# One-core encoder layer: four places for down weights, loads of experts 2 and 3 moved ahead, rows turned on VectorE, and one uniform expert loop

## What is computed

```python
x = x + mix @ w_out                        # after retention and differential attention
h = rmsnorm(x, norm_ffn)
# every token picks 1 of 4 groups, then 2 of the group's 4 experts (16 experts in all)
for e in its two experts:
    hid = silu(h @ w_gate[e]) * (h @ w_up[e])      # 1024 -> 512
    x  += weight[e] * (hid @ w_down[e])            # 512 -> 1024
gate = sigmoid(rmsnorm(x, norm_ple) @ w_ple_gate)
x = x + gate * (p @ w_ple_proj)
return rmsnorm(x, norm_final)
```

## Time and profile before

| | us |
|---|---|
| median of 3 runs | 639.49 (637.5 to 639.87) |
| the profiled execution, its time | 636.99 |
| the profiled execution, its span | 635.1 |
| TensorE busy | 589.0 (93%) |
| VectorE busy | 209.7 (33%) |
| ScalarE busy | 199.0 (31%) |
| GpSimd busy | 51.1 (8%) |

### The profile page before, as it was taken

One profiled execution on the slowest core, in us unless ns is written; L12 is line 12 of the kernel. 1 busy time (PEld: TensorE's weight loads), 2 busy tenths in 40 slices (PEclk: granted clock), 3 DMA queues, 4 the chain that ended last, 5 costly groups with the idle time before them and its releaser, 6 DMA issues.

```text
span 635.1 us, 9546 instructions
## 1 busy us (share of the span) xinstructions
PE 589.0 (93%) x3496; PEld 386.2 (61%) x3497; DVE 209.7 (33%) x460; ACT 199.0 (31%) x435; POOL 51.1 (8%) x89
## 2 busy tenths in 40 slices
PE   9999999999999999975769999999999987998994
PEld 9988777878988999974223333333333332335883
DVE  4521365456344342265101111011011010164753
ACT  5622254545443543240100010010010010073774
POOL 0000000000000000001101211211212211110000
PEclk9999999999999999995789999999999999998998
DMA  9852214213220249737994799999999999934001
GB/s 310 221 203 99 71 63 133 67 32 101 68 67 1 67 160 419 316 136 296 362 418 183 296 418 425 422 418 422 419 422 422 420 421 421 393 120 179 34 33 66
DMA packets 47232, 151.52 MB, mean 239 GB/s; under 512 B 7896, under 2 KB 27232, under 8 KB 34656
## 3 DMA queue, kind: packets, MB, share of 16 engines
q1 hardware_dynamic: 43520, 139.77, 56.3%
q0 software_dynamic: 3392, 11.02, 4.4%
q10 hardware_dynamic: 288, 0.29, 0.2%
HBM read 141.62 MB, written 9.45 MB: 238 GB/s over the span
## 4 chain that ended last, share of the span: by engine, by line
PE 83%; DMA 5%; DVE 4%; issue 3%; SPq 2%; ACT 2%; DVEq 0%; POOL 0%; ACTq 0%; POOLq 0%
PE bank L1622 19%; PE bank L1348 13%; PE bank L1349 12%; PE bank L1350 12%; PE bank L1648 10%; DMA ring_dn<-in_w_down 5%; PE bank L1430 2%; PE bank L1681 2%; SPq L586 2%; PE bank L1608 2%; PE bank L1403 2%; PE bank L1356 1%; PE bank L1634 1%; PE bank L1567 1%; PE bank L1444 1%
## 5 line engine op out<-in xcount | busy, mean ns | idle before, releaser
L1622 PE MATMUL bank<-ring_gu,rowsT 128*64 128x512 f32 (+1 forms) x800 | 144.7, 602 | 6.4 <-DMA ring_gu<-in_w_up 2.8
L1622 PEld LDWEIGHTS bank<-ring_gu,rowsT 128*64 128x64 f32 (+1 forms) x800 | 43.9, 128 | 92.4 <-issue 88.1
L1648 PE MATMUL bank<-ring_dn,hidT 128*64 128x512 f32 (+1 forms) x400 | 74.7, 607 | 9.8 <-issue 5.2
L891 ACT ACTIVATE silu_g<-bank 128x256 f32<-128x256 f32 x20 | 7.7, 384 | 221.8 <-PE bank L1622 221.8
L1087 DVE TENSOR_TENSOR w_lo<-w_raw,w_hi 128x2048 fp32r<-128x2048 f32 x17 | 39.0, 2293 | 76.7 <-ACT w_hi L752 64.9
L1246 DVE TENSOR_TENSOR hid<-silu_g,bank 128x256 f32<-128x256 f32 x20 | 8.4, 421 | 147.9 <-ACT silu_g L891 147.9
L1348 PE MATMUL bank<-w_hi,hT_hi 128*128 128x256 f32 x192 | 55.5, 289 | 0.8 <-issue 0.6
L1349 PE MATMUL bank<-w_lo,hT_hi 128*128 128x256 f32 x192 | 54.3, 283 | 0.0
L1350 PE MATMUL bank<-w_hi,hT_lo 128*128 128x256 f32 x192 | 54.3, 283 | 0.0
L1348 PE MATMUL bank<-hT_hi,w_hi 128*128 128x512 f32 x128 | 50.9, 397 | 0.1
L1648 PEld LDWEIGHTS bank<-ring_dn,hidT 128*64 128x64 f32 (+1 forms) x400 | 21.0, 128 | 48.4 <-issue 42.3
(11 more groups left out here) (217 smaller groups left out, 892.7 us busy)
## 6 DMA issues: line engine op xcount, KB each, us to landing
ring_gu<-in_w_gate SPq DMA_DIRECT2D x32, 1024.0 KB, 12.3
ring_gu<-in_w_up SPq DMA_DIRECT2D x32, 1024.0 KB, 15.3
ring_dn<-in_w_down SPq DMA_DIRECT2D x16, 2048.0 KB, 21.5
w_raw<-in_w_in SPq DMA_DIRECT2D x13, 1024.0 KB, 5.0
w_raw<-in_w_out SPq DMA_DIRECT2D x4, 1024.0 KB, 4.9
ple_gate_raw<-in_w_ple_gate SPq DMA_DIRECT2D x1, 4096.0 KB, 28.9
yg<-y_rows SPq DMA_DIRECT2D x8, 512.0 KB, 7.2
xr<-in_x SPq DMA_DIRECT2D x4, 512.0 KB, 8.8
```

Of the source, the lines that this page charges most:

```text
L1622: last = T.matmul(b_gu[q * BLK + t:q * BLK + t + n, :], rowsT[:, k % 4, k // 4, t:t + n], ring_gu[s][:, :, k, q * UC:(q + 1) * UC], start= ...
L1648: last = T.matmul(b_dn[q * BLK + t:q * BLK + t + n, :], hidT[:, kf % 2, kf // 2, t:t + n], ring_dn[s][:, kf, q * (D // 2):(q + 1) * (D // 2)],
```

## The change

It does these things.

- `ring_dn` gets a fourth place (`DN_AT` has four addresses, `GU_AT` three). Down of expert e + 1 is now loaded with gate-up of expert e. Gate-up 2 and down 3 are issued right behind the stores of `h2`, down 2 once the tables are ready. SP's loop over experts is written out, and in it each expert has gate-up e, then down e + 1, which waits for `dn_done` of the last block of expert e - 3. `ple_proj` is loaded behind the experts, `ple_gate_raw` in four pieces, and `gfin` last.
- The four row transposes and the two hidden transposes of TensorE, and the copies out of their banks, are gone. VectorE turns 32 by 32 squares instead: one instruction for a block's rows (`rows_turned`) and eight for its hidden values (`hidden_turned`). For this, `h2_rows` has four rows of 256 values for each token in place of two of 512, and a block is gathered by two indirect transfers.
- TensorE's code ahead of the loop and behind it is gone. The loop runs for all blocks and one turn more: turn t does `gate_up` of block t - 1 and `down` of block t - 2. In the first turn the code for `down` matches no copy. `one_of` is a chain of comparisons, one after the other, over six copies for `gate_up` and eight for `down`.
- The transposes of `p` stand behind the routing products, and `pair_weights` is done by VectorE after the first block's rows.

The diff, cut to its core:

```diff
+GU_AT = [107.75, 155.75, 16]
+DN_AT = [139.75, 187.75, 48, 0]
+N_GU, N_DN = len(GU_AT), len(DN_AT)
+
+
+CODE_DN, CODE_GU_LOADS, CODE_DN_LOADS = 8, 128, 1024
+NO_GU, NO_DN = 2 * N_GU, 2 * N_DN
...
-            def load_gu(e, slot, half):
+            def load_gu(e, half):
 
                 ks = slice(half * KD // 2, (half + 1) * KD // 2)
                 for n, w in enumerate((w_gate, w_up)):
-                    src = w[bass.ds(e, 1)].rearrange("o (q p j) f -> p (o q) j f", p=P, q=2)
-                    sp.dma_start(ring_gu[slot][:, n, ks, :], src[:, half]).then_inc(s_gu[slot][half], 16)
-
-            def load_dn(e, slot):
-                sp.dma_start(ring_dn[slot][:].rearrange("p (q j) n -> p q j n", q=2),
-                             w_down[bass.ds(e, 1)].rearrange("o (q p j) n -> p (o q) j n", p=P, q=2)).then_inc(s_dn[slot], 16)
+                    src = w[e].rearrange("(p h j) f -> p h j f", p=P, h=2)
+                    sp.dma_start(ring_gu[e % N_GU][:, n, ks, :], src[:, half]).then_inc(s_gu[e % N_GU][half], 16)
+
+            def load_dn(e):
+                sp.dma_start(ring_dn[e % N_DN][:],
+                             w_down[e].rearrange("(p j) n -> p j n", p=P)).then_inc(s_dn[e % N_DN], 16)
+
+            def blocks_through(e):
+                return sp.value_load(cum_i[0:1, e:e + 1], min_val=1, max_val=MAX_BLOCKS)
 
             for e in range(2):
-                load_gu(e, e, 0)
-                load_gu(e, e, 1)
-                load_dn(e, e)
-
-            sp.wait_ge(x1_add, NT * (OUT_UNITS - 1))
-            sp.dma_start(p_sb[:], p.rearrange("(t p) c -> p t c", p=P)).then_inc(s_pple, 16)
-            sp.dma_start(h2_rows[2 * SEQ:2 * SEQ + 2].rearrange("r (a c) -> (r a) c", c=BLK),
-                         small_tab[BLK:BLK + 2 * HALF // BLK, 0:BLK]).then_inc(s_h2, 16)
+                load_gu(e, 0)
+                load_gu(e, 1)
+                load_dn(e)
...
+            sp.dma_start(p_sb[:], p.rearrange("(t p) c -> p t c", p=P)).then_inc(s_pple, 16)
+            load_gu(2, 0)
+            load_gu(2, 1)
+
             sp.wait_ge(s_h2, 16 * (NT + 1))
+            load_dn(3)
+
+            sp.wait_ge(table_ready, 1)
             sp.wait_ge(p_T, D_PLE // P)
-            load_gu(2, 2, 0)
-            load_gu(2, 2, 1)
-
-
-            sp.wait_ge(table_ready, 1)
-            for buf in range(ROW_BUFS):
-                sp.wait_ge(s_rows[buf], 16)
-            load_dn(2, 2)
-            sp.dma_start(gfin[:], norm_final.rearrange("(o n) -> o n", o=1).to_broadcast([P, D])).then_inc(s_plegate, 16)
-
-            sp.wait_ge(x1_add, NT * OUT_UNITS)
...
+            for e in range(3, N_EXPERTS):
+
+                used = blocks_through(e - 3)
+                sp.wait_ge(gu_half_done, used)
+                load_gu(e, 0)
+                sp.wait_ge(gu_done, used)
+                load_gu(e, 1)
+                if e + 1 < N_EXPERTS:
+
+                    sp.wait_ge(dn_done, used)
+                    load_dn(e + 1)
+
+            sp.wait_ge(dn_done, blocks_through(N_EXPERTS - 4))
...
-            def reload_gu(e, slot):
-
-                used = blocks_through(e - RING)
-                sp.wait_ge(gu_half_done, used)
-                load_gu(e, slot, 0)
-                sp.wait_ge(gu_done, used)
-                load_gu(e, slot, 1)
-
-            def reload_dn(e, slot):
-
-                sp.wait_ge(dn_done, blocks_through(e - RING))
-                load_dn(e, slot)
-
-            reload_gu(RING, 0)
-            with sp.Fori(0, N_EXPERTS // RING - 1) as turn:
-                for n in range(RING):
-                    reload_gu(RING * turn + (RING + 1 + n), (n + 1) % RING)
-                    reload_dn(RING * turn + (RING + n), n)
-            reload_dn(N_EXPERTS - 1, 0)
...
-            def gather(buf, rows_of):
+
+            def gather(buf, table, first):
 
                 pool.sem_inc(gathers_begun, 1)
-                pool.indirect_dma_start(out=rows[buf][:], out_offset=None, in_=h2_rows,
-                                        in_offset=rows_of).then_inc(s_rows[buf], 16)
+                for g in range(2):
+                    rows_of = bass.IndirectOffsetOnAxis(ap=table[:, first + g:first + g + 1].bitcast(U32), axis=0)
+                    pool.indirect_dma_start(out=rows[buf][:, g, :], out_offset=None, in_=h2_rows,
+                                            in_offset=rows_of).then_inc(s_rows[buf], 16)
...
+            dve.sem_inc(y_ready, 2)
+            dve.sem_inc(hid_ready, 1)
+            dve.sem_inc(hidT_ready, 1)
 
             def hidden(b):
                 dve.wait_ge(sg_ready, b + 1)
+                if not isinstance(b, int) or b:
+
+                    dve.wait_ge(hidT_ready, b + 1)
                 V.tensor_tensor(hid[:], silu_g[:], b_gu[:, UC:2 * UC], ALU.mult).then_inc(hid_ready, 1)
 
-            def hiddenT(b):
-
-                dve.wait_ge(hT_done, b + 1)
-                V.tensor_copy(hidT[:], b_hT[:, 0:256].rearrange("p (j q t) -> p j q t", j=2, q=2)).then_inc(hidT_ready, 1)
+            def hidden_turned(b):
+
+                dve.wait_ge(hid_ready, b + 2)
+                for c in range(QUADS):
+                    q, g = divmod(c, 2)
+                    for h in range(2):
+                        last = V.transpose(hidT[(2 * q + h) * GRP:(2 * q + h + 1) * GRP, :, g * GRP:(g + 1) * GRP],
+                                           hid[c * GRP:(c + 1) * GRP, h * P:(h + 1) * P].rearrange("p (d m) -> p m d", m=4))
+                last.then_inc(hidT_ready, 1)
...
+            def rows_turned(b, buf, loads):
+
+                dve.wait_ge(s_rows[buf], 32 * loads)
+                if not isinstance(b, int) or b:
+
+                    dve.wait_ge(gu_done, b)
+                V.transpose(rowsT[:].rearrange("p k (g s) -> p g k s", g=2),
+                            rows[buf][:].rearrange("p g (d k) -> p g k d", k=KD)).then_inc(xT_ready, 1)
+
+            rows_turned(0, 0, 1)
+            pair_weights()
+            rows_turned(1, 1, 1)
             hidden(0)
+            hidden_turned(0)
             for b in range(2):
-                hiddenT(b)
+                rows_turned(b + 2, b, 2)
                 hidden(b + 1)
                 evacuate_y(b, b, fresh=True)
+                hidden_turned(b + 1)
 
             def step(b, k, turn):
-                hiddenT(b + 1)
+                rows_turned(b + 3, k % 2, (GROUP // 2) * turn + (k + 4) // 2 + 1)
                 hidden(b + 2)
                 evacuate_y(b + 1, k % 2)
+                hidden_turned(b + 2)
...
-            def step_code(b):
-                code = pe.value_load(blk_code[0:1, bass.ds(b, 1)], min_val=LOADS_0 + LOADS_1, max_val=8 * LOADS_1 - 1)
-                return code % LOADS_0, [code // LOADS_0 % (LOADS_1 // LOADS_0), code // LOADS_1]
-
-            def in_slots(b, products, pairs):
-
-                pair, loads = step_code(b)
-
-                def one_of(pairs):
-                    if len(pairs) == 1:
-                        products(pairs[0], loads)
-                        return
-                    first, rest = pairs[:len(pairs) // 2], pairs[len(pairs) // 2:]
-                    with pe.If(pair < 2 * rest[0][0] + (rest[0][0] != rest[0][1])):
-                        one_of(first)
+            def one_of(products, number, n, pair=0):
+
+                with pe.If(number == pair):
+                    products((pair // 2, (pair + 1) // 2 % n))
+                if pair + 1 < 2 * n:
                     with pe.Else():
-                        one_of(rest)
-
-                one_of(pairs)
+                        one_of(products, number, n, pair + 1)
...
-            def rows_transpose(buf, loads):
-
-                pe.wait_ge(s_rows[buf], 16 * loads)
-                for j in range(4):
-                    last = T.transpose(b_xT[:, j * P:(j + 1) * P], rows[buf][:, j::4], ident)
-                last.then_inc(xT_done, 1)
-
-            def gate_up(b, pairs=ANY):
-
-                def products(slots, loads):
-                    pe.wait_ge(xT_ready, b + 1)
+            def gate_up(turn, code):
+                loads = code // CODE_GU_LOADS % (CODE_DN_LOADS // CODE_GU_LOADS)
+
+                def products(slots):
+                    pe.wait_ge(xT_ready, turn)
+                    pe.wait_ge(hid_ready, turn)
...
-            rows_transpose(0, 1)
-
-            gate_up(0, pairs=[(0, 0), (0, 1)])
-            rows_transpose(1, 1)
-
-            def step(b, k, turn):
-                hidden_transpose(b - 1)
-                gate_up(b)
-                with pe.If(turn % ROW_BUFS < 1):
-                    rows_transpose(0, turn // ROW_BUFS + 2)
-                with pe.Else():
-                    rows_transpose(1, turn // ROW_BUFS + 2)
-                down(b - 1)
-
-            over_blocks(pe, total, step, group=1)
-            hidden_transpose(total - 1)
-            down(total - 1, pairs=[(0, 0), (2, 0)])
+                one_of(products, code // CODE_DN % (CODE_GU_LOADS // CODE_DN), N_DN)
+
```

(9 more changed lines are left out.)

260 lines of the change are left out of this document (129 added, 131 removed).

## The result

The changed kernel takes 644.4 us (median of 4 runs, 643.9 to 645.5), the kernel before 638.5 beside it: 1.0092 times as long, with an interval of 1.0073 to 1.0110. That is 5.9 us more, where I had said 3.9. I read places and durations from the profiles and differences of the whole from the medians.

A forecast was written before the change was run, and what follows sets the result against it. The prediction took the weight stream as the bound: its last unbroken run, from the end of `down(0)` (336.6), plus TensorE's 24.1 us behind it gave 565.2, +3.9 us, so 643.4 for the median; 8 in 10 from 635 to 649.5.

The forecast's parts named there:

- the likeliest case: At the loop's entry, two waits for late code one after the other: 641.5 to 647 us, chance 0.38.
- The bound: In the expert stage, transfers are the slower side: 16.5 us an expert, where TensorE wants 14.6.
- Routing and `gate_up(0)`: Ahead of the first block, wider tables and VectorE's turn: sum +0.5 us; `gate_up(0)` starts at 305.2, ends at 314.9.
- Entering the loop: Behind `gate_up(0)`, code waits until 314.6 and 320.5, then 3.3 us: `gate_up(1)` starts at 323.8, before 317.55.
- `down(0)` ends: After block 1's `gate_up` (9.2 us, low clock) and `down(0)` (3.6): end at 336.6, before 335.85.
- The stream: Weight loads from down 4 on: 204.3 us, kept fed by the fourth place; last piece in at 541.1.
- Behind the last piece: Work left after the last gate-up half: sum 24.1 us, experts end at 565.2 against 561.26, +3.9.
- At nothing: In the blocks, 22 us of removed TensorE transposes and the added VectorE turns lie under waits or products: no effect.
- Behind the experts: The tail behind 561 us keeps its two paths; no change was counted.
- The rule that I had weighed: Branches outside a two-page window force fetches; as last rival, every loop turn fetches: above 750 us, chance 0.02.

The follow-up runs named there:

- e3_dummy: Changed kernel with six 128x128 transposes, which nothing reads, at the head of every turn of TensorE's loop: 645.6 us.
- e7_short: Changed kernel with only the loop copies for one-expert blocks (3 `gate_up`, 4 `down`), the second expert of mixed blocks left out: 629.1 us.
- e8_walk: Changed kernel with TensorE walking once through its loop without products while VectorE still makes the table: 647.9 us.
- e2_peel: Changed kernel with `gate_up(0)` ahead of the loop again, with two copies, the loop beginning at its second turn: 640.4 us.
- e6_endswap: Changed kernel with gate-up 15 loaded ahead of down 15, all other loads in place: 640.2 us.
- e4_stage: Changed kernel with hidden values turned into a second buffer while `down` reads the first, then copied over: 642.2 us.
- e5_gu4first: Changed kernel with gate-up 4 loaded ahead of down 4, then down 5, the rest as before: 649.8 us.
- c2_release: c1_three with SP issuing every load in the order in which the places come free: 632.9 us.
- c3_order3: c1_three with gate-up ahead of down from gate-up 6 to 13, and the end as gate-up 14, gate-up 15, down 14, down 15: 627.0 us.
- c1_three: Changed kernel with the edits of e2_peel, e6_endswap and e4_stage together: 633.5 us.

## Why the prediction was right

The point was 643.4, its own range 641 to 648, and the likeliest case was the one that came. The places and the mechanism were right. That the point is only 1.0 us off is luck in part. The profiled execution I had put at 640.9, and it took 645.53, 4.6 more: 0.9 until the last piece is in, 2.9 behind it, 0.8 behind the experts. But I had set the median 2.5 above the profiled execution, as it was before, and it lies 1.1 below; that takes back 3.6. Step by step:

- **The bound.** Right, and shown by e3_dummy: work that TensorE loses or gains between 370 and 520 does not count.
- **Routing and `gate_up(0)`.** Start 306.45 for 305.2. The products with 56 columns took 7.07 in all where those with 28 took 7.03, so the 1 us that I had added for their width was nothing; the small VectorE operations took it up, for the table was ready at 303.5, as summed. From there 3.0 us passed, not 1.8: VectorE's turn of the rows began 1.6 us after the table with no wait shown, and took 1.10.
- **Entering the loop.** I had put 8.9 us of standing; it was 8.9, from 315.7 to 324.65, where I had its end at 323.8. The two long branches end at 314.9 and 320.7, for 314.6 and 320.5; the comparisons and the rest behind them took 3.9 for 3.3. That the branches wait for late code was an inference in the prediction; e7_short, e8_walk and the portions on q8 show it.
- **`down(0)` ends**: 337.56 for 336.6. `gate_up(1)` took 8.69 at the low clock, for 9.2.
- **The stream.** From down 4's issue to the last half of gate-up 15: 542.0 - 337.6 = 204.4 us, where 204.3 was worked out. The fourth place kept it fed, as said (share 1.02 from 353 to 370), but with little to spare: e2_peel ran dry at that very place. The sentence that the fourth place keeps the queue full holds only for an entry as slow as this one.
- **Behind the last piece** is the term that was mis-sized: 24.1 said, 27.0 measured. The four products before it came as said (3.64, 3.65, 7.04, 3.64). The gap was 4.20 us for 2.6: the eight turns on VectorE take 0.401 us each, not the 0.2 taken and above my upper end of 0.29, 1.6 us more; and `down(19)` took 5.12 for 3.65, 1.5 more, its clock down. I had taken the nearest row by its partitions and columns (128x128), but these turns have 32 partitions and 128 values each, and cost twice 0.2.
- **At nothing.** The 1.1 us row turn and 3.3 us of hidden turns a block are hidden in all blocks but the last. The only waits that the profile puts down to them are the one for the first block's rows and the 4.20 us ahead of the last `down`. The last block has no cover, and I had counted it with too small a price.
- **Behind the experts**, where I put nothing: from TensorE's leaving to the first transposes of the next stage 14.7 us (569.0 to 583.74), 13.9 before (561.26 to 575.17). Before, the chain goes there over TensorE's `ple_product`; now it goes over the last block's scatter and the load of `y_rows`, since `ple_product` ends at 582.9 and the residual sum is 0.8 us later. Only read, not tested.

Of the 8.5 us between the two profiles 1.7 are the end of `down(0)`, about 6.0 what comes from there to the end of the experts, 0.8 what lies behind. Seen from the end: the last weights of all landed at 544.5 before (down 15) and land at 542.0 now, so the unbroken stream did gain 2.5 us. But before only 16.8 us of the experts lay behind them, and now 27.0. Before, TensorE's last wait was for the piece ahead of the last, down 14, at 539.62; now it is for the last piece itself, 2.4 us later. That takes more than the gain; e6_endswap, which makes a down the last piece again, prices 4.2 us of it, and e4_stage 2.3.

The rule that I had weighed, of the Trainium skill, "Runtime: NRT & Kernel Launch", section "Instruction fetch mechanics", that a taken branch to a page not in the present window is a fetch, is what the first turns do here. Its window of two pages is not borne out: with 24 portions of instructions in the span (22 in the earlier trace rows) and no long branch behind the first turns, the loop's code stays through the rest of its 21 turns.

## What to carry to other kernels

Before an order of loads is changed, ask of each idle stretch of the transfer queue who else uses it: here code came through it, and filling it with weights cost more than it brought in e5_gu4first and won nothing in c2_release. c3_order3 asks for nothing earlier while the code comes and gained; part of its gain is the swap at the end. An edge of a stage is bought by what stands behind the last piece to land: let the piece with the least work behind it be the last. A cost that is hidden in every block but the last counts once, in full, with its clock.

## What I had not expected of the hardware

- Portions of code of 16 KB share the 16 transfer engines with the weights. With the transfers at a share of 0.07 they came some 3 us apart (330.2, 333.2, 336.5), with weights flowing 5.6 to 5.9 (e5_gu4first) or 6.3 (c2_release, 325.2 and 331.5). The same branch at the loop's entry waited 1.85 and 4.04 us, one at another place 3.31 and 6.20. No priority of code over weights is to be seen.
- VectorE's 32x32 turns of float32: 1.11 us for 128x512 and 0.401 for 32x128, where a copy of 128x512 takes 0.69.
- The granted clock of the last `down`, the 5 us behind a gap: 0.71 in the changed kernel after 4.20 us, but in two kernels with nearly the same gap 1.00 (e4_stage, 2.62) and 0.71 (c1_three, 2.59; in c2_release and c3_order3 0.67 after 2.57 and 2.56); in the kernel before 1.00 after two gaps of 1.26 and 0.88. The length of the gap alone doesn't tell. What brings it down there stays open.
